# Earlier places for the first expert lots, two lots in pieces, and the first expert's rows straight from the one-hot

## The chip, the cores and the metric

One core of a Trainium2 chip runs the whole kernel. The metric is device time in microseconds; the times given are medians over runs, and one more execution was recorded by the profiler.

## The reference

One layer of a decoder: 256 prompt tokens and 32 sample tokens (288 rows of 2048, f32) go through a mixer, a cross-attention and a mixture of experts. The change is in the last part:

```python
def hier_moe(n, ...):
    g_sel = argmax(softmax(x @ w_group + b_group))           # one of 4 groups
    top_w, top_i = top_k(softmax(e_logits of that group), 2) # two of its 4 experts
    for e in range(16):
        h = silu(x @ w_gate[e]) * (x @ w_up[e])              # 2048 x 512 each
        y = y + combine[:, e:e + 1] * (h @ w_down[e])        # 512 x 2048
```

Each expert's weights are 12.6 MB, all 16 together 201 MB, all in f32.

## The kernel before

The mixer and the cross-attention fill the first 683 us. The output projection of the cross-attention follows (`wo`, four column groups `c`, the router's products between them), then routing, then the 16 experts one after another (`for p in range(NEXP)` on TensorE, from line 1456 on). The residual rows are kept in `hx` ([token, 2048], three blocks of 128, 128 and 32 tokens), normed and turned back to rows by `turn_rows` (L1233).

**Lots.** An expert's weights come in six lots of 2 MB (`LOTS`: gate and up of the first half of the model columns, gate and up of the second half, down in two parts). Lot number is 6p + i. SyncE issues them in order (L549 to L556), each into one of nine places (`ring_at`, L386): six parts of `ring`, `nine`, a part of `XNN`, a part of `NC`. Lot n goes to place n % 9, and SyncE waits until the semaphore `moe_free` has reached n + 1. The first nine counts are given by TensorE before the experts begin: two after the mixer, two and one in the cross-attention (L1186, L1188), two after the last router products (L1213), two after the rank products of the routing (L1240). So lots 5 and 6 (places in `ring`, in which `wo` lay) wait for L1213, and lots 7 and 8 (`XNN`, `NC`) for L1240. From lot 9 on a place is free when TensorE has used up the lot in it: in `gate_up` after the eighth and the sixteenth step of the loop over `kt` (two lots each), in `down` after each half.

**An expert with 64 rows.** The gathered rows of a block (`xg`, two blocks, from DRAM by an indirect DMA of POOL) are turned by `rows_t` (L1272: the first of eight 128x128 turns is a plain product with the identity, the other seven are transposes; the slice is `i:D // 2:8`), VectorE multiplies them by the gain into `XT` (`lay_rows`, L2398), `gate_up` (L1320) makes 16 steps of two products, 64 rows by 512 columns, side by side in two column halves of the array. ScalarE takes Silu (L1931), VectorE the product (L2470), TensorE turns the hidden rows (`hidden_t`, L1395), ScalarE lays them (L1936), and `down` (L1402) follows. In the first expert the table of all slots is built after the eighth step (L1250) and the rows of expert 1 are turned between the halves of `down`.

**The first expert's rows.** They aren't gathered from DRAM. As soon as the one-hot `hot0` (token by slot) is made by VectorE (L2365), TensorE multiplies `hot0` as weights by `hx` (L1263, 12 products, 64x512 each), ScalarE copies the two banks to `xg` (L1924), then `block_rows_t(0)` turns them and VectorE lays them. A product `keep_clock(1)` (L1256, 128x512) stands before and after the turns.

Of the kernel before, what the change touches and what calls it, by code (L numbers as in the profile page):

```python
# [16 lines left out]
ALU = mybir.AluOpType  # L17
# [102 lines left out]
def decode_step(nc, consts, buckets, x_prompt, x_sample, cache_k, cache_v, cache_idx_k, cache_mem_k,  # L120
# [5 lines left out]
    with ctx:  # L126
# [256 lines left out]


        WHERE = (3, 4, 5, 2, 0, 1)
        ring_at = [ring[:, MSLOT * i:MSLOT * (i + 1)] for i in WHERE] + [XNN[:, 2352:2352 + MSLOT], NC[:, D:D + MSLOT]]  # L386
        ring_at.insert(4, nine[:, :])
        NRING = len(ring_at)
        gate_v, up_v = (w[0].rearrange("e (h p k) n -> e p h (k n)", h=2, p=128) for w in (w_gate, w_up))
        down_v = w_down[0].rearrange("e (p k) n -> e p (k n)", p=128)  # L390

# [120 lines left out]
        @block.sync  # L512
        def _(sp):
            for t in range(2):
                sp.dma_start(hx[:, t, :], x_prompt[0, t * 128:(t + 1) * 128, :]).then_inc(S(f"x_in{t}"), 16)
            sp.dma_start(hx[0:R, 2, :], x_sample.rearrange("b s d -> (b s) d")).then_inc(S("x_in2"), 16)
            n = 0
            for kind, c, wv in ITEMS + [("wo", c, wo_v[:, :, c * 512:(c + 1) * 512]) for c in range(4)]:
                if (kind, c) == ("out", 2):
                    rw = routeW.rearrange("p (k n) -> p k n", k=KT)  # L520
                    sp.wait_ge(S("routew_zero"), 1)
                    for cols, w in ((rw[:, :, 0:4], w_group), (rw[:, :, 4:20], w_router)):
                        sp.dma_start(cols, w[0].rearrange("(k p) n -> p k n", p=128)).then_inc(S("routew_in"), 16)
                    for cols, b in ((routeB[:, 0:4], b_group), (routeB[:, 4:20], b_router)):
                        sp.dma_start(cols, bass.AP(b.tensor, 0, [[0, 128], [1, b.shape[1]]])).then_inc(S("routew_in"), 16)
                if n == 0:
                    sp.dma_start(W80, wv).then_inc(S("w80_in"), 16)
                    n = 4
                    continue
                for q in range(4 if kind != "wo" else 1):  # L530
                    if n >= 2 * NSLOT:
                        sp.wait_ge(S("ring_free"), n - NSLOT + 1)
                    sp.dma_start(slot(n)[:, :, 0:wv.shape[2]], wv[:, 4 * q:4 * q + 4, :])\
                        .then_inc(S(f"ring_in{n % NSLOT}"), 16)
                    n += 1
                    if n == 9:
                        sp.wait_ge(S("x_laid_v"), 4)
                        sp.wait_ge(S("x_laid_a"), 8)
                        sp.dma_start(xts, C_).then_inc(S("xT_saved"), 16)
                        for t in range(2):  # L540
                            sp.dma_start(memX[:, t, :], mem_prompt[0, t * 128:(t + 1) * 128, :]).then_inc(S(f"mem_in{t}"), 16)


            sp.wait_ge(S("stored_in6"), 16 * 5)
            for e in range(NEXP):
                expert = e
                if e == NFIXED:
                    sp.wait_ge(S("hot_ready"), 3)
                if e >= NFIXED:  # L549
                    expert = sp.value_load(ids_order[:, e:e + 1], min_val=0, max_val=NEXP - 1)  # L550
                for i, (wv, part) in enumerate(LOTS):
                    lot = NL * e + i
                    sp.wait_ge(S("moe_free"), lot + 1)
                    if lot == 4:
                        sp.wait_ge(S("stored_mv0"), 16)
                    sp.dma_start(ring_at[lot % NRING], lot_of(wv, expert, part)).then_inc(S(f"moe_in{lot % NRING}"), 16)  # L556

            sp.wait_ge(S("route_ready"), 1)
            nov = sp.value_load(ids_nov, min_val=0, max_val=NOVF)
            sp.wait_ge(S("moe_free"), FREED)  # L560
            with sp.Fori(0, NOVF) as b:
                with sp.If(b < nov):
                    e = sp.value_load(ids[0:1, bass.ds(b + 91, 1)], min_val=0, max_val=NEXP - 1)
                    for i, (wv, part) in enumerate(LOTS):
                        sp.wait_ge(S("moe_free"), b * NL + (FREED - NL + i + 1))
                        sp.dma_start(ring_at[SPARE[i]], lot_of(wv, e, part)).then_inc(S(f"moe_in{SPARE[i]}"), 16)
            for n, (t, x) in enumerate(LAST):
                sp.wait_ge(S("y_ready"), n + 1)
                y, row = (y_prompt, t * 128) if t < 2 else (y_sample, 0)
                sp.dma_start(bass.AP(y.tensor, row * D + 512 * x, [[D, ROWS[t]], [1024, 2], [1, 512]]),  # L570
                             hx[0:ROWS[t], t, :].rearrange("p (h x c) -> p h x c", h=2, x=2)[:, :, x, :])\
                    .then_inc(S("y_stored"), 16)
            sp.wait_ge(S("y_stored"), 16 * len(LAST))
# [75 lines left out]
        def _(pe):  # L649
# [560 lines left out]
                last.then_inc(S("ring_free"), 1)  # L1210
                ring_n[0] += 1
            router(3).then_inc(S("r_sums"), 1)
            pe.nop().then_inc(S("moe_free"), 2)  # L1213
            pe.wait_ge(S("h_squares"), 4)
            for t in range(3):
                for sq in (sq_sum, sq_tmp):
# [20 lines left out]
            pe.wait_ge(S("picked"), 1)  # L1237
            for at, lhs, a, z in ((0, "rank", 0, 48), (16, "ones", 0, 32), (32, "ones", 0, 16)):
                last = mm(PS[:, 5, at:at + z - a], cc(lhs), AS[:, :, :].rearrange("p t e -> p (t e)")[:, a:z], start=at == 0, stop=at == 32)
            last.then_inc(S("moe_free"), 2)  # L1240
            for t in range(3):
                last = mm(PS[:, 5, 48:64], cc("ones"), AS[:, t, :], start=t == 0, stop=t == 2)
            last.then_inc(S("route_sum"), 1)
# [12 lines left out]
                    mm(PS[:, 6, :], ident, cst[:, 128:640], start=True, stop=True)  # L1256
            pe.wait_ge(S("row_out"), 12)
            pe.wait_ge(S("hot_ready"), 1)
            for x in range(2):
                for t in range(3):  # L1260
                    for half in range(2):
                        at = half * 1024 + x * 512
                        last = mm(PS[64 * half:64 * half + 64, 2 + x, :], hot0[0:ROWS[t], t, :], hx[0:ROWS[t], t, at:at + 512],  # L1263
                                  start=t == 0, stop=t == 2)
                last.then_inc(S("route_sum"), 1)
            keep_clock(1)

            def rows_t(k):
# [59 lines left out]
                              weights[c // 2][:, kt % 8, 256 * (c % 2):256 * (c % 2) + 256], start=kt == 0, stop=kt == KT - 1)  # L1328
                    yield last

            def gate_up(landed, between):

                for kt in range(KT):
                    if kt % 3 == 2:
                        between(kt // 3)
                    if kt % 8 == 0:
                        weights = lots_of(landed, kt // 8)
                    for last in full_products(XT, weights, kt):
                        if kt % 8 == 7:
                            last.then_inc(S("moe_free"), 1)  # L1340

            def star_gate_up(landed, between):

# [91 lines left out]
            def lots_at(p):  # L1435

                def landed(i):
                    lot = NL * p + i
                    pe.wait_ge(S(f"moe_in{lot % NRING}"), 16 * (lot // NRING + 1))
                    return ring_at[lot % NRING]  # L1440
                return landed

            def block_rows_t(b):

                if b:
                    pe.wait_ge(S(f"xg_in{b % 2}"), 16 * ((b + 1) // 2))
                    pe.wait_ge(S("xt_laid"), b)
                else:
                    pe.wait_ge(S("row_out"), 14)
                rows_t(b % 2).then_inc(S("xt_ready"), 1)  # L1450

            block_rows_t(0)
            keep_clock(1)

            def tables(s):

# [9 lines left out]
            for p in range(NEXP):  # L1466
                b, sub = block_of(p), sub_of(p)
                if p == PSTAR:
# [7 lines left out]
                    pe.wait_ge(S("ht_laid"), PSTAR + 2)  # L1476
                    star_down(lots_at(p))
                    continue
                pe.wait_ge(S("xt_laid"), b + 1)
                if p < NFULL - 1:  # L1480
                    gate_up(lots_at(p), gap(p))
                    if p:
                        block_rows_t(p + 1)
                    pe.wait_ge(S("hidden"), p + 1)
# [18 lines left out]
                if p == NEXP - 1:  # L1503
# [3 lines left out]
                    with pe.If(nov > 0):  # L1507
                        with pe.Fori(0, NOVF) as o:
                            with pe.If(o < nov):
                                def landed(i):  # L1510
                                    lots = len(range(SPARE[i], NLOT, NRING))
                                    pe.wait_ge(S(f"moe_in{SPARE[i]}"), o * 16 + 16 * (lots + 1))
                                    return ring_at[SPARE[i]]
                                pe.wait_ge(S("ov_x"), o * 16 + 16)
                                rows_t(1).then_inc(S("xt_ready"), 1)
# [27 lines left out]
        def _(act):  # L1543
# [375 lines left out]
                rows_out(g)  # L1919
            act.wait_ge(S("r_shifted"), 1)  # L1920
            A(RX, RX, ACT.Exp).then_inc(S("r_exp"), 1)
            for x in range(2):
                act.wait_ge(S("route_sum"), x + 2)
                A(xg[:, 0, 512 * x:512 * x + 512], PS[:, 2 + x, :], ACT.Copy).then_inc(S("row_out"), 1)  # L1924
            act.wait_ge(S("tab_ready"), 2)

            def full_silu(p):
# [59 lines left out]
        def _(dve):  # L1987
# [409 lines left out]
            def lay_rows(x=XT):  # L2397
                return TT(x, PSF[:, 0:1024].rearrange("p (i h r) -> p i h r", i=8, h=2), gain_x, ALU.mult)  # L2398
            dve.wait_ge(S("gcol_in"), 16)
            dve.wait_ge(S("xt_ready"), 1)  # L2400
            lay_rows().then_inc(S("xt_laid"), 1)
            own(TT(blk_hot, bc(cc("iota_r")[:, 0:NBLK], 1, [128, 6, NBLK]), bc(ids_blk, 2, [128, 6, NBLK]), ALU.is_equal))
            own(TT(row_hot, bc(cc("iota_r"), 1, [128, 6, CAP]), bc(ids_slot, 2, [128, 6, CAP]), ALU.is_equal))

# [14 lines left out]
            own(TT(who, who, bc(cc("iota_e", 1), 1, [1, 16, 16]), ALU.mult))  # L2419
            own(V.tensor_reduce(at_place, who, AXX, ALU.add))  # L2420
            V.tensor_copy(ids_order, at_place).then_inc(S("hot_ready"), 1)
            dve.wait_ge(S("route_sum"), 4)
            TS(tabS[:, :], PS[:, 7, 0:NBLK], 2.0, cc("half"), ALU.mult, ALU.add).then_inc(S("tab_ready"), 1)
            V.tensor_copy(tabF, PS[:, 7, 0:3 * NBLK]).then_inc(S("tab_ready"), 1)
            dve.wait_ge(S("tab_ready"), 2)
# [148 lines left out]
```

## Time and profile before

| | us |
|---|---|
| median of 3 runs | 1215.32 |
| lowest, highest run | 1207.06, 1216.66 |
| the profiled execution | 1210.47 |
| its span | 1208.6 |
| TensorE products busy | 1131.5 |
| VectorE busy | 471.1 |
| ScalarE busy | 186.6 |
| bytes read from HBM | 318.45 MB |

The profile is one execution. Times are from the start of the span. PE is a TensorE product, PEld its weight load (which overlaps products), DVE VectorE, ACT ScalarE, SPq SyncE's queue, which issues the weight transfers. An f32 product appears as two records, a transpose as one. Granted clock 1.00 is 2.4 GHz, 0.50 is 1.2 GHz.

### The profile page before, as it was taken

The page shows a single profiled execution, that of the slowest core. Times are in us where ns is not written, and L with a number is a line of the kernel's source. Part 1 is how long each engine was busy: PE and PEld are TensorE (multiplying, and loading weights), DVE is VectorE, ACT ScalarE, POOL GpSimd, SP SyncE. Part 2 cuts the span into 40 slices and gives each one's busy share as a digit, 9 for nine tenths or more (in the row PEclk, how much of TensorE's full clock was granted, in tenths as well). Part 3 has the DMA queues.
Part 4 walks back from the last instruction along what each step waited for, and adds up shares of the span by engine and source line. Part 5 has one row for each costly group of instructions (what it writes and reads, how often), then busy time and mean ns, then how long its engine had stood idle before and what let it go on. Part 6 is the DMA issues. An engine that isn't in the chain of part 4 may idle for free.

```text
span 1208.6 us, 14025 instructions
## 1 busy us (share of the span) xinstructions
PE 1131.5 (94%) x5834; PEld 555.5 (46%) x5834; DVE 471.1 (39%) x966; ACT 186.6 (15%) x401; POOL 48.8 (4%) x63
## 2 busy tenths in 40 slices
PE   7999999999999999999999999999999999959985
PEld 4334343344444455677777673333333333333332
DVE  5000069199565654011123465233333333412332
ACT  2103123200231243000022431000000000000010
POOL 0002000100000012100000001000000000000000
PEclk9999999999999999999999999899999999979998
DMA  8835623655342348854445739999999999999995
GB/s 294 289 129 131 184 86 124 226 174 174 105 137 91 124 184 336 290 145 139 139 158 218 283 116 406 397 415 426 428 426 427 427 425 429 425 427 427 426 427 227
DMA packets 71084, 327.60 MB, mean 271 GB/s; under 512 B 14006, under 2 KB 17878, under 8 KB 54444
## 3 DMA queue, kind: packets, MB, share of 16 engines
q1 hardware_dynamic: 55152, 282.65, 59.8%
q0 software_dynamic: 7888, 37.06, 8.1%
q10 hardware_dynamic: 7980, 6.99, 2.4%
q8 instruction: 47, 0.77, 0.3%
q14 instruction: 17, 0.14, 0.0%
HBM read 318.45 MB, written 10.49 MB: 272 GB/s over the span
## 4 chain that ended last, share of the span: by engine, by line
PE 80%; DVE 9%; DMA 6%; ACT 4%; issue 1%; DVEq 0%; POOL 0%; SPq 0%; ACTq 0%
PE PS L715 21%; PE PS L1042 16%; PE PS L1320 13%; PE PS L1402 7%; DMA ring<-in_w_up 5%; PE PS L1281 4%; PE PS L688 3%; PE PS L1327 2%; DVE X L2087 2%; DVE top L2086 2%; PE PS L1379 1%; PE PS L1285 1%; PE PS L1395 1%; PE PS L709 1%; DMA X<-in_x_prompt 1%
## 5 line engine op out<-in xcount | busy, mean ns | idle before, releaser
L715 PE MATMUL PS<-ring,NC 128*128 128x512 f32 x704 | 320.8, 600 | 1.8 <-issue 1.8
L715 PEld LDWEIGHTS PS<-ring,NC 128*128 128x128 f32 x704 | 128.7, 191 | 153.6 <-issue 152.0
L1042 PE MATMUL PS<-NC,ring 128*128 128x288 f32 x768 | 189.9, 407 | 1.6 <-DVE X L2244 0.5
L1320 PE MATMUL PS<-ring,NC 128*64 128x512 f32 x560 | 163.7, 605 | 7.4 <-DMA ring<-in_w_up 6.8
L1042 PEld LDWEIGHTS PS<-NC,ring 128*128 128x128 f32 x768 | 144.6, 190 | 42.4 <-issue 1.2
L2437 DVE TENSOR_TENSOR X<-X,PS 128x1024 f32<-128x1024 f32 x52 | 63.5, 1221 | 118.9 <-PE PS L1281 118.9
L1320 PEld LDWEIGHTS PS<-ring,NC 128*64 128x64 f32 x560 | 46.3, 138 | 101.3 <-issue 99.9
L1281 PE MATMUL PS<-XNN,NC 64*128 64x512 f32 x208 | 59.1, 645 | 1.4 <-DVE XNN L2475 0.8
L2244 DVE TENSOR_TENSOR X<-X,PS 128x288 f32<-128x288 f32 x16 | 7.3, 455 | 112.0 <-PE PS L1042 112.0
L1931 ACT ACTIVATE NC<-PS,small 64x512 f32<-64x512 f32 x11 | 7.5, 681 | 273.5 <-PE PS L1320 239.7
L1327 PE MATMUL PS<-ring,NC 128*32 128x256 f32 x384 | 36.0, 451 | 14.7 <-DMA ring<-in_w_up 14.7
L2086 DVE MAX8 top<-X 32x8 f32<-32x1028 f32 (+2 forms) x48 | 44.7, 931 | 1.0
L2087 DVE MATCH_REPLACE8 X<-top,X 32x1028 f32<-32x1028 f32 (+2 forms) x48 | 43.9, 914 | 0.0
L2440 DVE TENSOR_TENSOR X<-X,PS 32x1024 f32<-32x1024 f32 x26 | 31.5, 1210 | 27.4 <-PE PS L1285 27.2
L2113 DVE TENSOR_TENSOR ring<-small,cst 128x128 f32<-128x128 f32 x1 | 0.3, 291 | 105.0 <-ACT small L1655 105.0
L1402 PE MATMUL PS<-ring,NC 128*64 128x512 f32 x176 | 39.4, 595 | 0.0
L688 PE MATMUL PS<-ring,NC 128*32 128x512 f32 x288 | 38.4, 605 | 0.0
L1281 PEld LDWEIGHTS PS<-XNN,NC 64*128 64x128 f32 x208 | 15.9, 187 | 39.5 <-issue 25.6
L1327 PEld LDWEIGHTS PS<-ring,NC 128*32 128x32 f32 x384 | 18.7, 128 | 32.3 <-issue 27.7
L2475 DVE COPY XNN<-PS 128x1024 f32<-128x1024 f32 x11 | 13.5, 1225 | 44.7 <-PE PS L1402 32.1
L1852 ACT ACTIVATE NC<-X,gcol 128x288 f32<-128x288 f32 x16 | 8.6, 535 | 117.0 <-DVE X L2244 117.0
L634 POOL DMA_INDIRECT NC<-nsc,tabS x13 | 12.9, 995 | 331.2 <-PE PS L1272 281.6
(460 smaller groups left out, 1174.0 us busy)
## 6 DMA issues: line engine op xcount, KB each, us to landing
ring<-in_w_gate SPq DMA_DIRECT2D x27, 2048.0 KB, 19.7
ring<-in_w_up SPq DMA_DIRECT2D x22, 2048.0 KB, 17.1
ring<-in_w_in SPq DMA_DIRECT2D x36, 1024.0 KB, 5.1
ring<-in_w_down SPq DMA_DIRECT2D x16, 2048.0 KB, 18.6
ring<-in_w_out SPq DMA_DIRECT2D x16, 1024.0 KB, 5.1
nine<-in_w_down SPq DMA_DIRECT2D x6, 2048.0 KB, 22.0
XNN<-in_w_up SPq DMA_DIRECT2D x5, 2048.0 KB
NC<-in_w_gate SPq DMA_DIRECT2D x5, 2048.0 KB
```

Source lines behind the costliest of these rows:

```text
L688: last = mm(acc(n, 2)[32 * k:32 * k + 32, 0:width], lhs[:, 4 * q + k, T:NT], ws[:, k, 0:width], start=st, stop=sp_)
L715: last = mm(acc(n, t)[:, 0:width], lhs[:, kt, t * 128:(t + 1) * 128], slot(m)[:, k, 0:width], start=kt == 0, stop=kt == KT - 1)
L1042: last = mm(PS[:, j, 0:NT], slot(m)[:, k, 128 * j:128 * j + 128], src[:, kt, :], start=kt == 0, stop=kt == width * 4 - 1)
L1281: last = mm(PS[:, banks + half, :], slot_w[rows, k, 128 * t:128 * t + 128], ysb[rows, k, 512 * x:512 * x + 512], start=True, stop=True)
L1320: last = mm(PS[64 * half:64 * half + 64, 2, :], x[:, kt % 8, kt // 8, :], weights[half][:, kt % 8, :], start=kt == 0, stop=kt == KT - 1)
L1327: last = mm(PS[32 * c:32 * c + 32, bank, 0:256], x[:, kt % 8, kt // 8, STRIP * sub:STRIP * sub + STRIP], weights[c // 2][:, kt % 8, 256 * ...
L1402: last = mm(PS[64 * half:64 * half + 64, bank + x, :], hT[:, f, :], w[:, f % 2, half * 1024 + x * 512:half * 1024 + x * 512 + 512], start= ...
L2086: own(V.max(best, work))
L2087: own(V.match_replace(work, best, work, TAKEN))
L2437: return TT(out, out, PS[:, banks:banks + 2, :], ALU.add)
L2440: last = TT(out, out, PS[32 * x:32 * x + 32, banks:banks + 2, :], ALU.add)
L2475: V.tensor_copy(ysb[:, block_of(p) % 2, :], PSF[:, 2048:3072]).then_inc(S("y_out_psum"), 1)
```

## The change

1. The last two places change order: the part of `NC` takes lot 7, the part of `XNN` lot 8.
2. Lots 5 to 8 wait for what lay in their places instead of for counts of `moe_free`: lot 5 for two of the four column groups of `wo`, lot 6 for all four, lot 7 for the last router products, lot 8 for the last transpose of `turn_rows`.
3. Lots 9 and 10 come in four pieces each. TensorE reports the first three quarters of their places free after steps 1, 3 and 5 of the first expert's `gate_up`. The semaphore values that are waited for count the six further transfers (`landings`).
4. The first expert's rows are built turned: 48 products with slices of `hx` (every eighth column) as weights and `hot0` as the moving operand, straight into the layout of `XT`, then laid by VectorE in two halves. The two copies, the turns and one of the two `keep_clock` go away.
5. ScalarE loads the table of Silu ahead, right after the routing's Exp.

```diff
-        ring_at = [...] + [XNN[:, 2352:2352 + MSLOT], NC[:, D:D + MSLOT]]
+        ring_at = [...] + [NC[:, D:D + MSLOT], XNN[:, 2352:2352 + MSLOT]]
         ring_at.insert(4, nine[:, :])
         NRING = len(ring_at)
+        QUARTERED = (NRING, NRING + 1)
+        def landings(lot):
+            return 16 * (lot // NRING + 1 + 3 * (lot % NRING in [x % NRING for x in QUARTERED] and lot >= NRING))
...
-                    sp.wait_ge(S("moe_free"), lot + 1)
+                    if lot == QUARTERED[0]:
+                        for q in range(4):
+                            if q < 3:
+                                sp.wait_ge(S("quarter_free"), q + 1)
+                            for x in QUARTERED:
+                                wx, px = LOTS[x - NL * e]
+                                if q == 3:
+                                    sp.wait_ge(S("moe_free"), x + 1)
+                                sp.dma_start(ring_at[x % NRING][:, MSLOT // 4 * q:MSLOT // 4 * (q + 1)],
+                                             lot_of(wx, expert, px)[:, MSLOT // 4 * q:MSLOT // 4 * (q + 1)])\
+                                    .then_inc(S(f"moe_in{x % NRING}"), 16)
+                    if lot in QUARTERED:
+                        continue
+                    if lot in (5, 6):
+                        sp.wait_ge(S("ring_free"), 4 * (N_MQ + 1) + 2 * (lot - 4))
+                    elif lot == 7:
+                        sp.wait_ge(S("r_sums"), 1)
+                    elif lot == 8:
+                        sp.wait_ge(S("row_turned"), 12)
+                    else:
+                        sp.wait_ge(S("moe_free"), lot + 1)
...
             router(3).then_inc(S("r_sums"), 1)
-            pe.nop().then_inc(S("moe_free"), 2)
+            pe.nop().then_inc(S("moe_free"), 4)
...
-            last.then_inc(S("moe_free"), 2)
...
             pe.wait_ge(S("hot_ready"), 1)
-            for x in range(2):
-                for t in range(3):
-                    for half in range(2):
-                        at = half * 1024 + x * 512
-                        last = mm(PS[64 * half:64 * half + 64, 2 + x, :], hot0[0:ROWS[t], t, :], hx[0:ROWS[t], t, at:at + 512],
-                                  start=t == 0, stop=t == 2)
-                last.then_inc(S("route_sum"), 1)
+            for g in range(4):
+                for i in range(2 * g, 2 * g + 2):
+                    for h in range(2):
+                        for t in range(3):
+                            last = mm(PSF[:, 128 * i + 64 * h:128 * i + 64 * h + 64],
+                                      hx[0:ROWS[t], t, D // 2 * h + i:D // 2 * (h + 1):8], hot0[0:ROWS[t], t, :],
+                                      start=t == 0, stop=t == 2)
+                if g % 2:
+                    last.then_inc(S(("first_turned", "xt_ready")[g // 2]), 1)
             keep_clock(1)
...
-            def gate_up(landed, between):
+            def gate_up(landed, between, quarters=False):
                 for kt in range(KT):
+                    if quarters and kt == 4:
+                        pe.wait_ge(S("xt_laid"), 1)
...
+                    if quarters and kt in (1, 3, 5):
+                        last.then_inc(S("quarter_free"), 1)
...
-            block_rows_t(0)
-            keep_clock(1)
...
-            for x in range(2):
-                act.wait_ge(S("route_sum"), x + 2)
-                A(xg[:, 0, 512 * x:512 * x + 512], PS[:, 2 + x, :], ACT.Copy).then_inc(S("row_out"), 1)
+            act.preload_act_table(ACT.Silu)
...
-            dve.wait_ge(S("xt_ready"), 1)
-            lay_rows().then_inc(S("xt_laid"), 1)
+            for x, turned, laid in ((0, "first_turned", "first_laid"), (1, "xt_ready", "xt_laid")):
+                dve.wait_ge(S(turned), 1)
+                TT(XT[:, 4 * x:4 * x + 4, :, :], PS[:, x, :].rearrange("p (i h r) -> p i h r", i=4, h=2),
+                   gain_x[:, 4 * x:4 * x + 4, :, :], ALU.mult).then_inc(S(laid), 1)
```

## Rows read from the trace of the kernel before

**Rows 1.** The page's slices of the span, transfer engines, tenths of busy time

```profile
DMA  8835623655342348854445739999999999999995
```

**Rows 2.** Stretches: length, busy (count) PE, PEld, DVE, ACT, POOL; clock, DMA share, GB/s

```profile
700.00:718.00 18.00, 16.93 (x80) 11.78 (x78) 11.74 (x26) 4.81 (x9) 0.00 (x0) 1.00 0.00 0
719.00:778.00 59.00, 54.23 (x284) 25.14 (x285) 28.24 (x101) 10.03 (x19) 4.67 (x6) 0.94 1.00 409
778.00:780.00 2.00, 2.00 (x10) 0.44 (x6) 0.00 (x0) 0.00 (x0) 0.00 (x0) 1.00 0.54 229
792.00:1050.00 258.00, 255.30 (x1280) 88.64 (x1283) 98.04 (x90) 9.25 (x18) 7.89 (x8) 0.99 1.01 426
1050.00:1188.00 138.00, 111.90 (x1060) 48.28 (x1052) 38.96 (x43) 9.82 (x20) 0.99 (x1) 0.90 1.00 425
```

**Rows 3.** Timeline of SyncE's issues: start, us, line, transfer (lots 5, 9, 15)

```profile
718.14 0.33 SPq L556 DMA_DIRECT2D ring<-in_w_down  x1
...
744.75 0.33 SPq L556 DMA_DIRECT2D ring<-in_w_up  x1
...
...
779.06 0.33 SPq L556 DMA_DIRECT2D ring<-in_w_up  x1
```

**Rows 4.** Chain that ended last, from 1050 us: start, us, what

```profile
1051.56 31.78 DMA ring<-in_w_up
...
1156.19 26.43 DMA ring<-in_w_up
```

**Rows 5.** The same chain, 728 to 745 us, the first expert's rows

```profile
728.20 5.81 PE PS L1263 x24
734.01 1.06 PE PS L1256 x2
...
736.36 1.23 DVE NC L2398
737.64 7.09 PE PS L1320 x32
```

**Rows 6.** Timelines of weight loads: start, us until the last ends, line, shapes, count

```profile
720.58 5.18 PEld L1233 LDWEIGHTS PS<-cst,XNN 128*128 128x128 f32 x48
725.88 0.74 PEld L1239 LDWEIGHTS PS<-mkT,cst 128*128 128x128 f32 x6
734.71 0.31 PEld L1272 LDWEIGHTS PS<-cst,NC 128*128 128x128 f32 x1 [0.47 <-ACT NC L1924]
734.71 1.33 PEld L1272 LDWEIGHTS PS<-cst,NC 128*128 128x128 f32 x9 [0.47 <-ACT NC L1924]
735.73 0.30 PEld L1272 LDWEIGHTS PS<-cst,NC 128*128 128x128 f32 x2
1045.92 1.04 PEld L1372 LDWEIGHTS PS<-cst,NC 32*64 32x64 f32 x16 [1.62 <-DVE NC L2508]
```

**Rows 7.** Timeline of the strided weight loads of the turned hidden rows

```profile
757.06 0.88 PEld L1395 LDWEIGHTS PS<-cst,NC 64*128 64x128 f32 x5 [3.82 <-DVE NC L2470]
...
789.92 0.88 PEld L1395 LDWEIGHTS PS<-cst,NC 64*128 64x128 f32 x5 [0.34 <-DVE NC L2470]
```

**Rows 8.** Idle stretches and the clock: timelines, stretches (as rows 2), the chain

```profile
662.27 0.48 PE L1156 MATMUL PS<-mkT,NC 128*128 128x256 f32 x1 [2.19 <-ACT SQ L1876]
660.00:664.00 4.00, 1.81 (x23) 0.97 (x26) 3.69 (x22) 2.14 (x6) 0.53 (x1) 1.00 0.98 414
754.24 1.28 ACT L1931 ACT_TABLE_LOAD   x1 [19.58 <-PE PS L1320]
757.06 1.07 PE L1395 MATMUL PS<-cst,NC 64*128 64x64 f32 x5 [2.94 <-DVE NC L2470]
756.00:764.00 8.00, 6.46 (x19) 2.51 (x21) 0.76 (x1) 0.60 (x2) 0.00 (x0) 0.57 1.01 428
758.61 6.11 PE PS L1402 x16
766.16 3.58 PE PS L1402 x16
```

More of the change, by code:

```diff
@@ L385, in decode_step @@
         WHERE = (3, 4, 5, 2, 0, 1)
-        ring_at = [ring[:, MSLOT * i:MSLOT * (i + 1)] for i in WHERE] + [XNN[:, 2352:2352 + MSLOT], NC[:, D:D + MSLOT]]
+        ring_at = [ring[:, MSLOT * i:MSLOT * (i + 1)] for i in WHERE] + [NC[:, D:D + MSLOT], XNN[:, 2352:2352 + MSLOT]]
         ring_at.insert(4, nine[:, :])
         NRING = len(ring_at)
+        QUARTERED = (NRING, NRING + 1)
+        def landings(lot):
+            return 16 * (lot // NRING + 1 + 3 * (lot % NRING in [x % NRING for x in QUARTERED] and lot >= NRING))
         gate_v, up_v = (w[0].rearrange("e (h p k) n -> e p h (k n)", h=2, p=128) for w in (w_gate, w_up))
@@ L1438, in landed @@
                     lot = NL * p + i
-                    pe.wait_ge(S(f"moe_in{lot % NRING}"), 16 * (lot // NRING + 1))
+                    pe.wait_ge(S(f"moe_in{lot % NRING}"), landings(lot))
                     return ring_at[lot % NRING]
@@ L1443, in block_rows_t @@
             def block_rows_t(b):
[L1445 to L1449, printed above, removed]
+                pe.wait_ge(S(f"xg_in{b % 2}"), 16 * ((b + 1) // 2))
+                pe.wait_ge(S("xt_laid"), b)
                 rows_t(b % 2).then_inc(S("xt_ready"), 1)
-            block_rows_t(0)
-            keep_clock(1)
             def tables(s):
@@ L1478, in _ @@
                     continue
-                pe.wait_ge(S("xt_laid"), b + 1)
+                if p:
+                    pe.wait_ge(S("xt_laid"), b + 1)
+                else:
+                    pe.wait_ge(S("first_laid"), 1)
                 if p < NFULL - 1:
-                    gate_up(lots_at(p), gap(p))
+                    gate_up(lots_at(p), gap(p), quarters=p == 0)
                     if p:
@@ L1511, in landed @@
                                     lots = len(range(SPARE[i], NLOT, NRING))
-                                    pe.wait_ge(S(f"moe_in{SPARE[i]}"), o * 16 + 16 * (lots + 1))
+                                    pe.wait_ge(S(f"moe_in{SPARE[i]}"), o * 16 + landings(SPARE[i] + NRING * lots))
                                     return ring_at[SPARE[i]]
@@ L2421, in _ @@
             V.tensor_copy(ids_order, at_place).then_inc(S("hot_ready"), 1)
-            dve.wait_ge(S("route_sum"), 4)
+            dve.wait_ge(S("route_sum"), 2)
             TS(tabS[:, :], PS[:, 7, 0:NBLK], 2.0, cc("half"), ALU.mult, ALU.add).then_inc(S("tab_ready"), 1)
```

## The prediction

> **What bounds the kernel now.** I read the slices of the page first, then the stretches, then SyncE's transfer issues, then the chain and TensorE around the change. In the last 40% of the span the transfer engines are busy almost without a break [rows 1]. The stretches give it in numbers: nothing moves from 700 to 718 us; from 719 to 778 the sixteen engines are full at 409 GB/s; from 778 to 780 their share is 0.54; from 792 to 1188 it is 1.00 again at 425 to 426 GB/s [rows 2]. One lot is 2 MB, so it takes 4.9 us at 426 GB/s. An expert has six lots, 29.5 us, and its token gather is on top.
>
> At first sight each microsecond of transfer brought forward into the idle 700 to 718 is a microsecond won at the end. The issues say otherwise [rows 3]. Lots 5 and 6 go out at 718, 9 and 10 at 745, and lot 15, which waits for its place until TensorE is halfway through the second expert's gate and up products, at 779.06. The share fell to 0.54 in just that stretch: all that had been issued had landed, and the transfers stood still until TensorE released a place. So up to 779 the stream follows TensorE, whatever was loaded before. From there it is never empty again, and it sets the end: the chain waits 31.8 and 26.4 us for w_up late in the kernel [rows 4]. The end moves with the moment at which lot 15 is issued, and that moves with TensorE's start on expert 1 (769.7).
>
> **TensorE at the first expert.** Lots 5 to 10 issued earlier, in four pieces or not, are therefore worth nothing at the end by themselves: lots 5 and 6 were in before TensorE asked for them (the chain has its first long wait for a transfer at 1051 [rows 4]), and 9 to 14 are all in by 778. I cost the loading half of the change at nothing. The cover is the drained queue at 779; were it gone, the worth would be one lot moved into the idle stretch, 4.9 us. The eight quarter transfers and their waits stand on SyncE's queue, behind which only later lots wait, and those are released later anyway. What counts is TensorE's own time from the one-hot to expert 1.
>
> *Removed:* 12 one-hot products (24 passes), two copies by ScalarE, 8 transposes, one 128x1024 evacuation by VectorE and one of two clock-keeping products. They are one chain from 728.20 to the start of gate and up at 737.64 [rows 5]: 9.4 us.
>
> *Added:* 8 x 2 x 3 = 48 products. An f32 product is two passes in the records, each with its own weight load (3 products at L1239 make six loads), so 96 loads and 96 passes with 64 moving columns. A pair of halves with 512 moving columns takes 0.44 us a pass (L1320, 32 in 7.09 us [rows 5]), so 64 columns stream in 0.055 us; the load of 128 weight columns is longer and sets the pace. Contiguous weights go at 0.108 us each (48 in 5.18 us) or 0.11 (six in 0.74) [rows 6]. But the new weights are `hx[..., i::8]`, one element in eight. Strided loads stand in the trace too. At L1272 (stride 8 as well) the load of the first product, the only one there that is no transpose, lasts 0.31 us. Nine loads run from 734.71; the last two start at 735.73 and, one transpose's pace later, at 735.84; taking 0.108 for each of six transposes, the two passes have 1.13 - 0.65 = 0.48 us, 0.24 each. At L1372 (stride 4, 64 columns) eight pairs of loads take 1.04 us, 0.13 a pair; without the tail of the last pair, taken as 0.13, (1.04 - 0.13) / 8 = 0.114 us for 64 columns, 0.23 for 128 [rows 6]. A plain doubling of 0.108 would be 0.216. I take 0.225, with ends 0.216 and 0.24: 96 x 0.225 = 21.6 us (20.7 to 23.0). One clock-keeping product of two 512-column passes, 0.9 us, stays. Gate and up need the first half of the rows, laid long before, and the second from their fifth step on, 3.5 us after their start; its 0.6 us evacuation (half of 1.23 [rows 5]) is hidden there. Stage: 21.6 + 0.9 - 9.4 = +13.1 us (12.2 to 14.5).
>
> *The clock.* In this stage TensorE's array would stand between short passes, waiting for loads. The trace shows its clock falling from 2.4 to 1.2 GHz after it stood: after the 2.9 us idle at 754 the mean granted clock of 756 to 764 is 0.57, and 16 down products take 6.11 us where the next 16 take 3.58 [rows 8], 2.5 us lost. No row shows how it takes many short waits; I expect such a fall here. The strided loads themselves should not get longer: the loads at L1395, also strided, take 0.88 us together at 757 (low clock) and at 790 (full) [rows 7]. What is lost is the start of the dense products after it, +2.5 us (0 to 3.4).
>
> *Given back.* The table load for Silu, 1.28 us in the chain between gate-up and down [rows 8], goes to where ScalarE is free: -1.3 us. The idle there shrinks to 1.7 us. A 2.2 us idle at 660 left the clock at 1.00 [rows 8], so I take the 2.5 us of the slow down products as won back as well (0 to 2.5; the same phase could still fall). Then lots 11 to 14 come closer behind each other than before, and lot 15 may find the queue not quite empty: about +0.5 us (0 to 1).
>
> **The sum.** 13.1 + 2.5 - 1.3 - 2.5 + 0.5 = +12.3 us, on the profiled execution's 1210.5: 1222.8. The median of the three runs, 1215.3, is 4.8 above that execution, so as a median I forecast 1227.5. Ends of this case: 12.2 + 0 - 1.3 - 2.5 = +8.4 and 14.5 + 3.4 - 1.3 + 1 = +17.6, that is 1223.7 and 1232.9 as medians.
>
> **Rivals.** (a) *The stride costs nothing* (the other side, not slower). If weight loads keep the contiguous pace, the stage is 96 x 0.108 + 0.9 - 9.4 = +1.9; the clock then holds, as it does over the 5.2 us of transposes at that pace, so +1.9 - 3.8 + 0.5 = -1.4 us, 1213.9. For it: the transposes at L1272 are strided too, and turns at such a stride hide in the 1.33 us of nine loads. Against it: each of these is one pass with 128 moving columns, which can hide its load, while the true products at L1272 and L1372 show 0.23 to 0.24. It decides below 0.125 us a load (96 x 0.125 = 12.0, where the sum is zero). Chance 0.09.
> The Trainium skill ("TensorE: Matmul & The Clock Gate", LDWEIGHTS (loading the stationary operand)) has a load last its columns divided by 1.2, without a word on stride; that would be 107 ns for 128 columns and would give this rival's time. By that rule, the contiguous loads agree and the strided ones above do not.
> (b) *The transfers decide from the start.* Then one lot moved into the idle 18 us gives -4.9 us, 1210.4. For it: share 1.00 from 719 to 778. Against it: 0.54 at 778 to 780. Chance 0.05.
> (c) *Strided loads do double at the low clock.* After some 3 us the remaining 80 or so take 0.45 each: 80 x 0.225 = 18 us more, 1245. Against it: L1395. Chance 0.06.
> (d) My case, chance 0.80. If the quarters (rows of 4 KB instead of 16) ran slower, nothing would follow, since the stream waits for TensorE at 779.
>
> **How the numbers follow.** The range takes the likeliest case widened at both ends by the spread of the runs (1207 to 1217): 1219 to 1236; it leaves out (a), (b) and (c), the first two below it and the third above. About what a measurement can tell from no change is 1%, 12.2 us. My case stands on that bound: half of its 0.80 is above, and (c) too: 0.46 slower. The other half, (a) and most of (b) are within 1%: 0.49. Faster by over 1% is left with 0.05.
>
> **What would show it.** The 48 products' loads at about 0.22 us each and the stage some 21 us long; at 0.11 and 10 us (a) holds; at 0.45, (c). Lot 15's issue later by about the same 12 us as the end. Transfers idle for ten microseconds before the first quarters are released, and this without effect. No table load between the first gate-up and down, and the first expert's down at 3.6 us for both halves. Granted clock below 1 somewhere from 730 to 755. I am wrong if lot 15 is issued earlier than 779, or if the end does not follow it.

## The result: slower, by more than forecast

The changed kernel takes 1236.3 us (median, 1234.5 to 1238.1) against 1212.8 for the kernel before in the runs beside it; ratio 1.0198, 95% interval 1.0149 to 1.0246. The forecast was 1227.5 (1219 to 1236) beside 1215.3. The chances were 0.49 for within 1%, 0.46 for slower and 0.05 for faster. The direction was that of the forecast's central sum, and TensorE was what decided, as forecast; but the loss is 23.5 us instead of 12.2, about twice as much, and lies outside the range.

The page of the changed kernel, slices of the span for TensorE's clock and the transfer engines:

```profile
PEclk9999999999989999999999985999999999989998
DMA  8836533555333368754456661999999999999995
```

Where rows 1 had a transfer share of 3 in slice 24 and full slices from 25 on, slice 25 is now nearly empty (1), and the clock line shows 8 and 5 in slices 24 and 25. The stretches (columns as in rows 2), ahead of the stage, in it, at lot 15 and after it:

```profile
706.00:721.00 15.00, 15.00 (x72) 10.41 (x70) 9.59 (x21) 3.75 (x7) 0.00 (x0) 1.00 0.29 122
741.00:769.00 28.00, 28.00 (x90) 21.62 (x92) 6.26 (x23) 0.00 (x0) 0.00 (x0) 0.51 0.12 52
803.00:805.00 2.00, 2.00 (x10) 0.43 (x6) 0.61 (x1) 0.00 (x0) 0.00 (x0) 1.00 1.03 442
818.00:1075.00 257.00, 254.31 (x1284) 88.64 (x1288) 97.92 (x90) 9.26 (x18) 7.92 (x8) 1.00 1.01 427
1075.00:1214.00 139.00, 110.96 (x1060) 46.72 (x1052) 39.08 (x43) 10.03 (x21) 0.99 (x1) 0.89 1.00 424
```

Lot 5 does move in the stretch in which nothing moved before. But from 741 to 769 the transfers have 12% to do: they wait for the first quarters, that is for TensorE, which stands in the 48 products at half clock. From 818 on the stretches are those of before (258 and 138 us at 426 and 425 GB/s [rows 2]), only later.

SyncE's issues (start, us, line, transfer): lot 5, lot 8, the first quarter, lot 14, lot 15.

```profile
704.02 0.33 SPq L581 DMA_DIRECT2D ring<-in_w_down  x1
...
733.42 0.33 SPq L581 DMA_DIRECT2D XNN<-in_w_gate  x1
769.17 0.33 SPq L566 DMA_DIRECT2D ring<-in_w_up  x1
...
795.96 0.33 SPq L581 DMA_DIRECT2D ring<-in_w_gate  x1
805.10 0.33 SPq L581 DMA_DIRECT2D ring<-in_w_up  x1
```

Lot 15 goes out at 805.10 instead of 779.06 [rows 3]: 26.0 us later. The span is 1234.4 instead of 1208.6: 25.8. The end followed lot 15.

The chain through the stage (start, us, what), beside rows 5 and 8. L1287 are the 48 products, L1280 is keep_clock, L1346 gate and up (L1320 before), L1274 the table of slots (L1250 before), L1432 down (L1402 before):

```profile
735.45 28.84 PE PS L1287 x96
764.29 2.01 PE PS L1280 x2
766.29 7.99 PE PS L1346 x32
774.28 2.38 PE PS L1274 x24
776.66 7.07 PE PS L1346 x32
...
787.10 3.65 PE PS L1432 x16
...
795.79 1.72 PE PS L1346 x8
```

From the first one-hot product to expert 1 it is 60.3 us; before, it was 769.7 - 728.2 = 41.5. The change's own part is +18.8 us. The other 7.3 of the profiled 26 lie ahead of the stage, which begins at 735.45 instead of 728.20; they are taken up at the end of the section on the forecast.

### The profile page after: what moved, and what is told of

It is laid out like the page before. It is cut to its first block, busy times and chain, and to the rows that moved or that the text cites. A ratio compares the mean times of both kernels' runs of the same rounds, so it can differ in the third digit from the quotient of the medians.

```text
span 1234.4 us, 14152 instructions
## 1 busy us (share of the span) xinstructions
PE 1156.5 (94%) x5895; PEld 580.4 (47%) x5895; DVE 471.3 (38%) x967; ACT 185.9 (15%) x399; POOL 48.9 (4%) x63
## 4 chain that ended last, share of the span: by engine, by line
PE 79%; DVE 8%; DMA 6%; ACT 4%; issue 1%; ACTq 1%; DVEq 0%; POOL 0%; SPq 0%
PE PS L740 20%; PE PS L1067 15%; PE PS L1346 13%; PE PS L1432 6%; DMA ring<-in_w_up 5%; PE PS L1307 4%; PE PS L713 3%; PE PS L1353 2%; PE PS L1287 2%; DVE X L2112 2%; DVE top L2111 2%; PE PS L1409 1%; PE PS L1311 1%; PE PS L1425 1%; DMA X<-in_x_prompt 1%
## 5 line engine op out<-in xcount | busy, mean ns | idle before, releaser
L740 PE MATMUL PS<-ring,NC 128*128 128x512 f32 x704 | 324.9, 607 | 1.8 <-issue 1.8
L1346 PE MATMUL PS<-ring,NC 128*64 128x512 f32 x560 | 164.8, 609 | 8.4 <-DMA ring<-in_w_up 8.4
L1346 PEld LDWEIGHTS PS<-ring,NC 128*64 128x64 f32 x560 | 46.6, 139 | 104.5 <-issue 104.4
L1432 PE MATMUL PS<-ring,NC 128*64 128x512 f32 x176 | 39.4, 595 | 0.0
L1307 PEld LDWEIGHTS PS<-XNN,NC 64*128 64x128 f32 x208 | 15.9, 187 | 39.5 <-issue 25.5
L1287 PE MATMUL PS<-natS,X 128*128 128x64 f32 (+1 forms) x96 | 28.8, 456 | 0.8 <-DVE natS L2390 0.8
L1287 PEld LDWEIGHTS PS<-natS,X 128*128 128x128 f32 (+1 forms) x96 | 25.1, 326 | 4.4 <-issue 0.9
```

Source lines behind the costliest of these rows:

```text
L740: last = mm(acc(n, t)[:, 0:width], lhs[:, kt, t * 128:(t + 1) * 128], slot(m)[:, k, 0:width], start=kt == 0, stop=kt == KT - 1)
L1287: last = mm(PSF[:, 128 * i + 64 * h:128 * i + 64 * h + 64], hx[0:ROWS[t], t, D // 2 * h + i:D // 2 * (h + 1):8], hot0[0:ROWS[t], t, :], st ...
L1307: last = mm(PS[:, banks + half, :], slot_w[rows, k, 128 * t:128 * t + 128], ysb[rows, k, 512 * x:512 * x + 512], start=True, stop=True)
L1346: last = mm(PS[64 * half:64 * half + 64, 2, :], x[:, kt % 8, kt // 8, :], weights[half][:, kt % 8, :], start=kt == 0, stop=kt == KT - 1)
L1432: last = mm(PS[64 * half:64 * half + 64, bank + x, :], hT[:, f, :], w[:, f % 2, half * 1024 + x * 512:half * 1024 + x * 512 + 512], start= ...
```

## Experiments

### Which half does it: e1 and e2

e1 takes the new rows back and keeps everything else:

```diff
-            for g in range(4):
-                for i in range(2 * g, 2 * g + 2):
...
+            for x in range(2):
+                for t in range(3):
+                    for half in range(2):
...
+            block_rows_t(0)
+            keep_clock(1)
...
+                A(xg[:, 0, 512 * x:512 * x + 512], PS[:, 2 + x, :], ACT.Copy).then_inc(S("row_out"), 1)
```

> The change without its part 4: places, early lots, quarters and the early Silu table stay, the first expert's rows are built as before. Theory A (the 48 products alone make the kernel slower): the stage from the first one-hot product to gate and up takes 9.4 us again, expert 1's gate and up start no later than before, and the end is at or a little under before, 0 to -4 us (table load 1.3 us and the slow down products 2.5 us won back). Theory B (the early lots or the pieces cost something too): some 5 us or more slower than before, with the stage at 9.4 us.

Measured: 1213.0 against 1215.4, ratio 0.9981 (0.9947 to 1.0014). e2 is the kernel before with the new rows alone.

> The kernel before with part 4 alone; no early lots, no quarters, no early table. Theory A: stage about 31 us instead of 9.4, the end 19 to 24 us later than before, at most 4 us above the whole change (the table load is back). Theory B: clearly less than the whole change's 23 us, say under 15.

Measured: 1236.6 against 1215.4, ratio 1.0161 (1.0109 to 1.0213); its 96 passes take 28.95 us and it starts expert 1 64.9 us after the first of them. The whole loss comes with part 4; the loading half, the quarters and the early table don't slow anything that the runs can show. Of the two gains expected of e1 only the table load came: the clock fell in the gap all the same, and the first half of down took 6.58 us.

### What the 96 passes cost: stride, changes of row count, clock (e3, e4, e10 to e12)

e3 takes neighbouring columns as weights:

```diff
-    hx[0:ROWS[t], t, D // 2 * h + i:D // 2 * (h + 1):8], hot0[...]
+    hx[0:ROWS[t], t, D // 2 * h + 128 * i:D // 2 * h + 128 * i + 128], hot0[...]
```

> The whole change with the 48 products' weights taken from 128 neighbouring columns of hx instead of every eighth; the columns of the first expert's input are then in another order, so its part of the output is another one. Same count, same shapes. If the stride sets the price, loads go at 0.11 us instead of 0.24, 96 loads take 10.5 us plus some 4 to 6 us for the 32 changes between 128-row and 32-row weights, stage 15 to 18 us instead of 31, end 12 to 15 us earlier than with the change. If it is the clock or the count of products, the stage stays above 25 us.

Measured: 1233.5, ratio 1.0151 (1.0098 to 1.0204). The products' entry in its chain of waits:

```profile
730.74 25.52 PE PS L1287 x96
```

A stretch within them, columns as in rows 2:

```profile
733.00:756.00 23.00, 23.00 (x85) 19.82 (x84) 4.86 (x20) 0.00 (x0) 0.00 (x0) 0.50 0.43 181
```

With keep_clock the stage is 25.5 + 2.0 = 27.5 us, not 15 to 18: the other branch of the expectation (above 25 us, the clock or the count) is the one that came. The weight loads of this run, and then of the change (ns min/median/max):

```profile
L1287 PEld LDWEIGHTS PS<-natS,X x96: 181/333/333, 730.7 to 755.7; 128*128 128x128 f32 x64, 32*128 32x128 f32 x32
```

```profile
L1287 PEld LDWEIGHTS PS<-natS,X x96: 307/332/337, 735.4 to 763.8; 128*128 128x128 f32 x64, 32*128 32x128 f32 x32
```

The contiguous loads begin at 181 ns and end at 333, as long as the strided ones: the clock is at 0.50 for the whole stretch. So in this stage the stride cost only 28.8 - 25.5 = 3.3 us, because a contiguous load at the low clock takes almost what a strided one takes at either.

e4 puts two 32-row products side by side:

```diff
-                        for t in range(3):
+                        order_t = (2, 1, 0) if h else (0, 1, 2)
+                        for t in order_t:
...
-                                      start=t == 0, stop=t == 2)
+                                      start=t == order_t[0], stop=t == order_t[2])
```

> The whole change, the three token blocks taken in the order 0,1,2 and 2,1,0 by turns, so that two 32-row products stand side by side: 16 changes between 128-row and 32-row weights instead of 32 (same sums, other order). If each change costs about 0.2 us (loads 0.40 to 0.45 us apart there, 0.24 elsewhere), the 28.8 us of products become 25 to 26 and the end comes about 3 us earlier. If the pace is a matter of the mean load only, 28.8 us stay.

Measured: 1234.3, ratio 1.0161 (1.011 to 1.0213). The products in the chain:

```profile
731.57 26.06 PE PS L1288 x96
```

16 changes of row count fewer, 28.84 - 26.06 = 2.8 us less, 0.17 us for each. That is as expected in the profile; the time of the runs can't show it. Nearly all these changes stand at a clock of 0.50. In the trace of the change only two came before the clock fell: there the weight loads start 0.40 us apart, at the later ones 0.45. So a part of the price may be that of the low clock; no run has many changes at full clock.

e12 leaves out the 32-row block, strided weights as in the change:

```diff
-                        for t in range(3):
+                        for t in range(2):
```

> The whole change with its strided weights, the third token block left out of the products (sample tokens missing from the first expert's rows): 64 passes of 128 rows. Strided loads at 0.238 us whatever the clock: 64 x 0.238 = 15.2 us. Set against the change's 28.8 us for 96 passes with 32 changes of row count, the difference is 32 x 0.238 = 7.6 for the passes and the rest, 6.0, for the changes, 0.19 us each.

Measured: 1222.3, ratio 1.0061 (1.0036 to 1.0086), and in the chain

```profile
730.02 15.52 PE PS L1287 x64
```

That is 0.24 us a pass, nearly all at a clock of 0.50. The seven loads before the clock fell start 0.22 to 0.24 us apart, the later ones 0.24, and the two passes at L1272 at full clock were 0.24 apart too [rows 6]: the pace of the strided loads doesn't depend on the level of the clock. The change's 28.8 us are then 96 x 0.24 = 23.0 and 5.8 for the 32 changes of row count, 0.18 each, in agreement with e4.

e10 is e12 with neighbouring columns as weights, e11 besides moves 128 columns of a constant into another bank. The edit of e11 against the change:

```diff
-                        for t in range(3):
-                            last = mm(PSF[:, 128 * i + 64 * h:128 * i + 64 * h + 64],
-                                      hx[0:ROWS[t], t, D // 2 * h + i:D // 2 * (h + 1):8], hot0[0:ROWS[t], t, :],
...
+                        for t in range(2):
+                            last = mm(PS[:, 2 + h, 0:128],
+                                      hx[0:ROWS[t], t, D // 2 * h + 128 * i:D // 2 * h + 128 * i + 128], cst[0:ROWS[t], 128:256],
...
```

> The whole change with neighbouring columns as weights and the third token block (32 rows) left out of the 48 products: 32 products, 64 passes, all of 128 rows, 64 moving columns. The sample tokens are missing from the first expert's rows and their columns are in another order. No change of row count is left. If the clock falls all the same, a load takes 0.213 us, 64 x 0.213 = 13.6 us; if it holds, 64 x 0.11 = 7.0 us. Theory D (the waits at the changes of row count bring the clock down): it holds. Theory E (short passes behind long loads bring it down): it falls.

> As the run before, but 128 columns of a constant are moved by each product, into a bank that nobody reads, so that a pass is as long as its load; the first expert's input isn't computed. Both theories let the clock hold here: 64 x 0.11 = 7.0 us, keep_clock 0.9 to 1.1, gate and up at full clock from the start. If it falls here too, neither is right.

The products in the chain of e10:

```profile
727.57 12.03 PE PS L1287 x64
```

and a stretch within them:

```profile
730.00:741.00 11.00, 11.00 (x47) 9.83 (x47) 6.03 (x23) 0.00 (x0) 0.00 (x0) 0.50 0.59 251
```

The products in the chain of e11:

```profile
735.17 9.01 PE PS L1287 x64
```

and two stretches around and within them:

```profile
735.00:740.00 5.00, 4.83 (x29) 4.86 (x30) 4.35 (x21) 0.90 (x1) 0.00 (x0) 0.66 1.00 411
740.00:744.00 4.00, 4.00 (x38) 4.00 (x37) 2.62 (x11) 0.00 (x0) 0.00 (x0) 1.00 1.03 438
```

e10 ran at 1.003 (1.0003 to 1.0058), e11 at 0.9959 (0.9929 to 0.9989). e10 has no change of row count, and its clock falls as well, 2.0 us into the products, and stays down to their end: the waits at those changes are not needed for the fall (theory D is out). Its loads start 0.11 us apart before the fall and 0.213 after it.

e11 missed its expectation, 9.0 us instead of 7.0, and by that expectation's own words neither theory passes: the clock fell here too, 0.7 us into the products (735.9). But after 3.4 us it was back at 1.00 and stayed there, with loads 0.11 us apart. So long passes didn't prevent the fall, and what brought it about isn't shown; what e10 and e11 show is whether the clock came back while the products ran. Between the two the moved columns doubled, but what is moved changed with them (the one-hot is nearly all zeros, half of this constant's entries are ones), and so did the bank written. Which of these brought the clock back wasn't separated; the width is only the likeliest.

### Does a wider operand save the change? e5 and e6

> As the flat run (weights from neighbouring columns), but each of the 48 products moves 128 columns of a constant instead of the 64 of the one-hot, into a bank that nobody reads; the first expert's input isn't computed. More work per product. Flat with 64 columns took 25.5 us with the clock at 0.50 from its second microsecond on and 0.213 us a load. Theory C (the fall of the clock is the larger part of the price): if the clock holds here, loads go at 0.11 us, and with 0.26 at each of 32 changes of row count the 96 take about 15 us, 10 less than flat although they move twice the columns; the end is some 12 us before flat's. If the clock falls here too, or is not the cause, 25 us or more.

> The whole change with its strided weights, but 256 moving columns of a constant instead of the one-hot's 64, into a bank that nobody reads; the first expert's input isn't computed. Strided loads were 0.238 us apart at both levels of the clock. So if the stride alone sets the pace, the 96 products take 26 to 29 us here too (0.24 each and 0.4 at a change of row count), even with the clock at 1.00; only keep_clock (0.9 instead of 2.0 us) and the start of gate and up (7.1 instead of 8.0) get shorter, end 2 to 3 us before the change's. If strided loads too are slowed by the low clock, the 96 fall to 20 us or less.

e5 is e3 with the operand of e11, e6 the change with 256 columns of the constant. Measured: e5 1232.6, ratio 1.016 (1.0112 to 1.0207); e6 1258.5, ratio 1.0371 (1.0329 to 1.0414). For e5 the branch with the clock held (about 15 us) missed and the other branch (25 us or more) came; for e6 neither branch did (26 to 29 us, or 20 and less). The products in the chain of e5, then those of e6:

```profile
733.45 28.45 PE PS L1287 x96
```

```profile
732.60 50.49 PE PS L1287 x96
```

A stretch within e6's:

```profile
735.00:785.00 50.00, 50.00 (x93) 27.15 (x92) 6.51 (x25) 0.00 (x0) 0.00 (x0) 0.50 0.19 81
```

With the 32-row products in the order, the clock fell and stayed low for 50 us although a pass of 256 columns lasts longer there than its load: the passes of 128 rows start 0.43 us apart, and 64 of them alone make 27 of the 50 us. e11 differs from e5 only in that it has no 32-row products, and there the clock came back; e5 moves the same constant, so the constant alone doesn't bring it back. So the clock stayed down with 64-column passes without any 32-row products (e10), and with 32-row products between the others even with 128 and 256 columns (e5, e6). Which property of the 32-row products does that, the quarter of the rows or the longer spacing at the changes, wasn't separated.

### Does TensorE's delay reach the end? e7

```diff
-            keep_clock(1)
+            keep_clock(13)
```

> The kernel before with 12 more keep_clock products (13 instead of 1) between the one-hot products and the turns: 12 x 0.86 = 10.3 us more on TensorE at full clock, nothing else. If TensorE's delay reaches the end in full (lot 15 waits for it at 779), gate and up of expert 1 and lot 15 come 10.3 us later and the end 10 us later (ratio 1.008). If the transfers decide, as the rival had it, the end moves by under 3 us.

Measured: 1224.4, ratio 1.0106 (1.007 to 1.0142), which holds the expected 1.008. Lot 15 in its trace:

```profile
790.08 0.33 SPq L556 DMA_DIRECT2D ring<-in_w_up  x1
```

In that trace lot 15 goes out 11.0 us later than before and the end comes 9.9 us later. Lot 15 against the end of the span, over kernels whose ends lie 50 us apart:

| | first one-hot product | lot 15 | end of span | lot 15 to end |
|---|---|---|---|---|
| before | 728.2 | 779.1 | 1208.6 | 429.5 |
| the change | 735.5 | 805.1 | 1234.4 | 429.3 |
| e2, new rows alone | 731.2 | 805.4 | 1235.4 | 430.0 |
| e7, 10.3 us more on TensorE | 729.2 | 790.1 | 1218.5 | 428.4 |
| e6, 256 columns | 732.6 | 827.4 | 1257.5 | 430.1 |
| e8, filler, with early lots | 730.5 | 777.7 | 1206.0 | 428.3 |
| e9, filler, without early lots | 734.7 | 782.0 | 1215.0 | 433.0 |

In the seven kernels not listed (e1, e3 to e5, e10 to e12) it is 427.8 to 430.1 us as well.

### A faster version, and what the loading half is worth: e8 and e9

```diff
+                    if p == 0:
+                        keep_clock(2)
                     pe.wait_ge(S("hidden"), p + 1)
```

> The change without part 4 (old rows), and two keep_clock products of 0.86 us put into the first expert's idle time between its up products and the turn of the hidden rows. In the profile without them the clock fell at 759 for 6.8 us and the first half of down took 6.58 us instead of 3.6. If the filler holds the clock, that half takes 3.6 us, expert 1 starts 3 us earlier after the stage, and the end is 3 to 5 us before the kernel before (ratio 0.996 to 0.998). If the clock falls anyway: no difference from the run without filler.

Measured: 1210.9 against 1213.6, ratio 0.9978 (0.9958 to 0.9998). Gap and down in the chain of e8:

```profile
756.40 1.91 PE PS L1280 x4
758.32 0.96 PE PS L1421 x5
759.74 3.65 PE PS L1428 x16
```

Two useless products (L1280) stand in the gap and the clock holds; the first half of down takes 3.65 us instead of e1's 6.58, and from the first one-hot product to expert 1 it is 37.9 us instead of 41.5. It is 0.2% faster than the kernel before, with 1 just outside its interval. Against e1 (0.9981 without the filler) the runs can't tell them apart; what the filler does is shown by the profile.

> The kernel before with two things only: the early Silu table and the two keep_clock products in the first expert's idle time; no early lots, no pieces, old rows. Same as the filler run but for the loading half (places, early lots, quarters). If the loading half is worth nothing while the transfers wait for TensorE at lot 15, this run's stage, lot 15 to end (428 to 430 us) and time are those of the filler run within 2 us. If the loading half brings something, this one is 3 to 5 us slower.

Measured: 1213.9 against 1215.1, ratio 0.9978 (0.9961 to 0.9995), so in time the two can't be told apart. In the profile they can. Stretches of e8 and then of e9 around lot 15:

```profile
776.00:778.00 2.00, 2.00 (x10) 0.59 (x8) 0.25 (x1) 0.00 (x0) 0.00 (x0) 1.00 0.97 418
778.00:780.00 2.00, 2.00 (x10) 0.48 (x8) 1.18 (x1) 0.00 (x0) 0.00 (x0) 1.00 0.96 262
```

```profile
780.00:782.00 2.00, 2.00 (x12) 0.54 (x8) 0.51 (x1) 0.00 (x0) 0.00 (x0) 1.00 0.96 410
782.00:784.00 2.00, 2.00 (x10) 0.67 (x12) 0.93 (x1) 0.00 (x0) 0.00 (x0) 1.00 1.00 426
```

e8 shows the dip (262 GB/s) right behind the issue of lot 15 at 777.7, where before had one too (229 GB/s [rows 2]): what had been issued was all but done, and the rate is low while the new lots begin. e9 has no such dip: its transfers still have a backlog there, and lot 15 to end is 433.0 instead of 428.3, 4.7 us or one lot (4.9 us) longer. e9's issues of lot 5 and lot 15:

```profile
724.68 0.33 SPq L556 DMA_DIRECT2D ring<-in_w_down  x1
...
781.99 0.33 SPq L556 DMA_DIRECT2D ring<-in_w_up  x1
```

From lot 5 to the end it is 1215.0 - 724.7 = 490.3 us in e9, and 1208.6 - 718.1 = 490.5 before [rows 3]. In e9, with TensorE 3.6 us faster, the transfers decide from lot 5 on, and the lot moved into the idle stretch counts; and the kernel before stood within about a microsecond of that limit. That this is real in time rests on one profile of each.

## Why the forecast was right in kind and wrong in size

**What bounds the kernel: right.** The end follows lot 15 within 2 us in every kernel of the table but e9, where TensorE was fast enough for rival (b). Rival (b) is out for the change: its transfers stood almost idle for 28 us and the end didn't notice more than TensorE's delay.

**The loading half at nothing: right.** e1 stands at 0.9981 with it. Its cover was the dry queue at 779, priced at one lot if gone; e9 shows 4.7 us.

**The 48 products: the step that failed.** The sum had 96 x 0.225 = 21.6 us, ends 20.7 and 23.0. The pace between products of equal rows was 0.24 (e12), so 23.0, the upper end. Missing was a whole term: going from a 128-row to a 32-row block and back, 32 times, 0.18 us each, 5.8 us (28.8 less 23.0; e4: 0.17 each). The forecast counted instructions of one kind and put their order at nothing. The trace of before could have warned: its 12 one-hot products go through the same blocks, and their starts are 0.43 us apart between equal rows (729.08 to 729.51) and 0.52 where 128 and 32 rows meet (729.54 to 730.06, 730.55 to 731.07). That is 0.09 us a change beside long passes; the 0.18 beside short ones it doesn't show. That the price is there is shown by e4 and e12; why a change costs it, and how much of it is the low clock's, stays open.

**The clock: right to expect, right in price for this kernel.** It fell at 737.5 and stayed at 0.50 to the first dense products. Paid were 1.0 us in keep_clock (2.01 instead of 1.06 [rows 5]) and 0.9 in the first half of gate and up (7.99 instead of 7.09 [rows 5]): 1.9 against the 2.5 of the sum. It fell 0.7 to 2.1 us into the products in all nine kernels that have them, short or long, strided or not, and in none with the old rows (before, e1, e7 to e9); why, no run shows. Rival (c), loads doubling at the low clock, is out for strided loads (0.24 at either level), but the pace of contiguous ones does just that: 0.11 to 0.213 us in e10.

**What was given back: right.** In the change no table load stands in the gap and down took 3.65 us; from the end of up to expert 1 12.0 us instead of 15.5, 3.5 less against 3.8 in the sum. That the down products came back is luck: in nine kernels with the early table and no filler in the gap, the clock fell there in five (e1, e3, e4, e6, e12; 5.35 to 6.58 us for the first half of down) and held in four (the change, e5, e10, e11; 3.65 us).

**Rival (a), the stride costs nothing,** would have been wrong twice: the strided pace is there, and without it the clock would have taken most of the gain (e3: 25.5 us).

**The sum against the trace.** Forecast 13.1 + 2.5 - 3.8 = 11.8 for the stage up to expert 1; measured 18.8. Of the 7.0 missing, 5.8 are the changes of row count and 1.4 the pace, less 0.2 for smaller differences. 18.8 us are a ratio of 1.0155, inside the measured interval, near its lower end.

**The rest, 7.3 us in the profiled pair.** The stage begins at 735.45 instead of 728.20. The code ahead of it is the same but for when lots 5 to 8 are issued. e10 has the same early lots and begins at 727.57, e9 without them at 734.73. So the early lots don't do it. The stretches from the start of the span to the stage, before and the change:

```profile
0.00:728.20 728.20, 693.65 (x3154) 392.03 (x3154) 300.68 (x754) 161.03 (x352) 35.90 (x50) 0.99 0.53 179
0.00:735.45 735.45, 700.78 (x3154) 396.70 (x3154) 300.74 (x754) 162.59 (x353) 35.92 (x50) 0.98 0.54 182
```

The same 3154 product records take TensorE 7.1 us more, at a mean clock of 0.98 instead of 0.99 (e10: 1.00); VectorE's time is the same. The clock falls at other moments in the earlier part of each execution, and the beginning of the stage wanders by 8 us among these kernels. That also bounds what one trace can carry: e2's stage is 4.6 us longer than the change's, it begins 4.2 us earlier, and the two medians differ by 0.3 us.

The range was drawn from the case's bounds and the runs of before and had no term for this. With the stage right the sum would have been 1227.5 + 7.0 = 1234.5, and a range as wide as the stated one around it would have held the measured 1236.3.

## What to carry to other kernels

Before pricing a stage of TensorE by count and duration, write down the order of its operands: a change of the number of weight rows between neighbours cost 0.18 us each here, 32 of them in 96 passes, at a price that no single row shows. The rebuild, which replaced few long products by many short ones, also gave up the clock here, and at the low clock contiguous weights (25.5 us) were hardly better than strided ones (28.8 us). And before moving transfers forward, look where the queue runs dry: what lies ahead of that point was not on the path here until the engine that releases the places got faster.

## What the hardware showed that I had not expected

- A contiguous f32 load of 128 columns went from 181 to 333 ns in one stage when the clock fell to 0.50 (e3); a strided one is 307 to 337 ns at both levels (the change).
- Between a 128-row and a 32-row product of the same columns 0.17 to 0.18 us are lost each way (64 moving columns, clock mostly at 0.50).
- The clock stayed at 0.50 for 50 us with TensorE busy in every microsecond of it (e6: 256-column passes, 32-row products among them), where in e11 it came back 3.4 us after it fell.
